# The gate phase of PEER: started 32 gathered rows earlier on VectorE, with two of three steps' gated comparison made by ScalarE

## What is computed

```
s = einsum('thcd,hcnd->thcn', q, sub_keys)            # 8 heads, 2 halves, 128 keys
s_top, i_top = top_k(s, 16)                           # then top 16 of the 256 sums
best_s, best_pos = top_k(cand_s, 16)
expert = take_along_axis(cand_e, best_pos)            # i0 * 128 + i1, out of 16384
gate = softmax(best_s)
act = gelu(einsum('td,thkd->thk', x, u[expert]))
y = einsum('thk,thkd->td', gate * act, v[expert])
```

## Time and profile before

| | us |
|---|---|
| median of 3 runs | 5255.7 |
| lowest, highest | 5235.42, 5274.73 |
| profiled execution, its own time | 5254.98 |
| span of its trace, first to last instruction | 5253.1 |

### The profile page before, as it was taken

One profiled execution on the slowest core, in us unless ns is written; L12 is line 12 of the kernel. 1 busy time (PEld: TensorE's weight loads), 2 busy tenths in 40 slices (PEclk: granted clock), 3 DMA queues, 4 the chain that ended last, 5 costly groups with the idle time before them and its releaser, 6 DMA issues. The chain is left out here.

```text
span 5253.1 us, 56097 instructions
## 1 busy us (share of the span) xinstructions
PE 4308.1 (82%) x21158; PEld 3533.7 (67%) x21158; DVE 3096.9 (59%) x5685; ACT 1026.1 (20%) x2272; POOL 1920.2 (37%) x1559
## 2 busy tenths in 40 slices
PE   6989679788997559996787799996888997469995
PEld 5467438577886458885555688863677886458884
DVE  1315540599957796656216633345599867796656
ACT  0102310222332150000012222211222332150000
POOL 0000230166657624444002433312256557614444
PEclk9985669899998779998878788858899998779997
DMA  2330112488889948998111000013588889939998
GB/s 91 89 75 1 34 37 96 167 301 313 311 338 397 369 128 342 409 396 348 56 58 35 1 1 1 1 41 104 188 300 310 319 341 390 363 109 371 409 399 333
DMA packets 403487, 1099.26 MB, mean 209 GB/s; under 512 B 70508, under 2 KB 157261, under 8 KB 402886
## 3 DMA queue, kind: packets, MB, share of 16 engines
q0 software_dynamic: 186496, 679.04, 34.4%
q1 hardware_dynamic: 216726, 416.69, 22.6%
HBM read 1066.88 MB, written 32.45 MB: 209 GB/s over the span
## 5 line engine op out<-in xcount | busy, mean ns | idle before, releaser
L1036 DVE SCALAR_TENSOR_TENSOR gg_ytok<-gg_ring,gg_gw,gg_ytok 128x1024 f32<-128x1024 f32 x320 | 422.1, 1319 | 178.5 <-DMA gg_ring<-in_peer_v,gg_idx 172.5
L1036 DVE SCALAR_TENSOR_TENSOR fg_ytok<-fg_ring,fg_gw,fg_ytok 128x1024 f32<-128x1024 f32 x320 | 422.0, 1319 | 176.6 <-DMA fg_ring<-in_peer_v,fg_idx 170.0
L706 POOL DMA_INDIRECT fg_ring<-in_peer_u,fg_idx x320 | 377.2, 1179 | 351.7 <-DVE fg_ring L1030 284.4
L706 POOL DMA_INDIRECT gg_ring<-in_peer_u,gg_idx x320 | 374.4, 1170 | 345.7 <-DVE gg_ring L1030 275.9
L1030 DVE SCALAR_TENSOR_TENSOR fg_ring<-fg_ring,fg_htok 128x1024 f32<-128x1024 f32 x320 | 409.7, 1285 | 128.1 <-DMA fg_ring<-in_peer_u,fg_idx 126.4
L1030 DVE SCALAR_TENSOR_TENSOR gg_ring<-gg_ring,gg_htok 128x1024 f32<-128x1024 f32 x320 | 409.8, 1286 | 127.8 <-DMA gg_ring<-in_peer_u,gg_idx 125.7
L774 PE MATMUL fg_bank<-f_hTd,fg_uT 128*128 128x256 f32 x2048 | 476.9, 387 | 0.6 <-ACT f_buf L873 0.6
L774 PE MATMUL gg_bank<-g_hTd,gg_uT 128*128 128x256 f32 x2048 | 476.2, 387 | 0.6 <-ACT g_buf L873 0.6
L706 POOL DMA_INDIRECT gg_ring<-in_peer_v,gg_idx x320 | 358.1, 1119 | 272.1 <-DVE gg_ytok L1036 211.8
L706 POOL DMA_INDIRECT fg_ring<-in_peer_v,fg_idx x320 | 345.7, 1080 | 276.3 <-DVE fg_ytok L1036 214.4
L774 PEld LDWEIGHTS fg_bank<-f_hTd,fg_uT 128*128 128x128 f32 x2048 | 389.8, 196 | 51.2 <-issue 0.9
(11 more groups left out here) (620 smaller groups left out, 7758.8 us busy)
## 6 DMA issues: line engine op xcount, KB each, us to landing
fg_ub<-in_peer_u SPq DMA_DIRECT2D x128, 512.0 KB, 6.8
gg_ub<-in_peer_u SPq DMA_DIRECT2D x128, 512.0 KB, 6.7
fg_ub<-in_peer_v SPq DMA_DIRECT2D x64, 512.0 KB, 7.2
fg_uT<-in_peer_v SPq DMA_DIRECT2D x64, 512.0 KB, 6.7
gg_ub<-in_peer_v SPq DMA_DIRECT2D x64, 512.0 KB, 7.3
gg_uT<-in_peer_v SPq DMA_DIRECT2D x64, 512.0 KB, 6.8
f_buf<-in_peer_w_q SPq DMA_DIRECT2D x16, 1024.0 KB, 12.2
g_buf<-in_peer_w_q SPq DMA_DIRECT2D x16, 1024.0 KB, 11.8
```

Source lines behind the costliest of these rows:

```text
L706: pool.indirect_dma_start(ring[:, n % RING, :], None, (u_rows if kind == "u" else v_rows)[:, :], bass.IndirectOffsetOnAxis(ap=idx[:, r:r + ...
L1036: dve.scalar_tensor_tensor(ytok[:, :], row, gw[:, r:r + 1], ytok[:, :], ALU.mult, ALU.add).then_inc(used, 1)
```

## The change

Four edits, all in PEER. `UNITS_U` falls from 370 to 338, so the gate phase stands 32 gathered units earlier in DVE's order, and 32 more units stand after it. `place` uses 30 us in place of 25 for the Gelu over dots. In steps with `t % 3 != 2` (22 of 32) DVE makes only the first comparison; ACT builds the second one with its gate: eight `Abs` (distance of `iota128` from the index, L896 in the changed file) and, after a wait for its own writes, eight `Relu` of gate minus gate times distance (L902), which is the gate where the distance is 0 and 0 elsewhere. For that `selT` gets a fourth part, the negated gate. PE waits for both DVE and ACT before a step.

```diff
-UNITS_U = 370
+UNITS_U = 338
...
-        selT = ph.sb("selT", [P, 3, TD])
+        selT = ph.sb("selT", [P, 4, TD])
...
+        def by_act(t):
+            return t % 3 != 2
...
-        for c, k in zip(early_chunks, place(sched, [dots_at[c] for c in early_chunks], 25.0)):
+        for c, k in zip(early_chunks, place(sched, [dots_at[c] for c in early_chunks], 30.0)):
...
                 for t in range(NGC):
                     pe.wait_ge(og_done, t + 1)
+                    pe.wait_ge(oh_done, t + 1)
...
-                    act.activation(selT[:, :, i * P:(i + 1) * P], acc[:, i, 0:3 * P].rearrange("p (a t) -> p a t", a=3),
-                                   ACT.Copy).then_inc(sT_done, 1)
+                    act.activation(selT[:, 0:3, i * P:(i + 1) * P], acc[:, i, 0:3 * P].rearrange("p (a t) -> p a t", a=3),
+                                   ACT.Copy)
+                    act.activation(selT[:, 3, i * P:(i + 1) * P], acc[:, i, 2 * P:3 * P], ACT.Copy, scale=-1.0
+                                   ).then_inc(sT_done, 1)
...
-                    act.wait_ge(oh_done, t + 1)
-                    for k in range(GT):
-                        a = oh[t % 2][:, 1, k, :]
-                        last = act.activation(a, a, ACT.Copy, scale=selT[:, 2, t * GT + k:t * GT + k + 1])
-                    last.then_inc(og_done, 1)
+                    if by_act(t):
+                        if t >= 2:
+                            act.wait_ge(gm_done, t - 1)
+                        elif t == 0:
+                            act.wait_ge(g_done, nblk)
+                        for k in range(GT):
+                            last = act.activation(oh[t % 2][:, 1, k, :], iota128, ACT.Abs, scale=-1.0,
+                                                  bias=selT[:, 1, t * GT + k:t * GT + k + 1])
+                        last.then_inc(ab_done, 1)
+                        act.wait_ge(ab_done, sum(by_act(x) for x in range(t + 1)))
+                        for k in range(GT):
+                            a, col = oh[t % 2][:, 1, k, :], slice(t * GT + k, t * GT + k + 1)
+                            last = act.activation(a, a, ACT.Relu, scale=selT[:, 3, col], bias=selT[:, 2, col])
+                        last.then_inc(og_done, 1)
+                    else:
...
-                    for a in range(2):
+                    for a in range(1 if by_act(t) else 2):
```

More of the change, by code:

```diff
@@ L523, in peer_layer @@
                                                          ph.sem("hit_done"), ph.sem("look_done"))
-        idx_done, gate_done, sT_mm, sT_done = ph.sem("idx_done"), ph.sem("gate_done"), ph.sem("sT_mm"), ph.sem("sT_done")
+        idx_done, gate_done, sT_mm, sT_done, ab_done = ph.sem("idx_done"), ph.sem("gate_done"), ph.sem("sT_mm"), ph.sem("sT_done"), ph.sem("ab_done")
         t_half, e_half, h_done, g_done = ph.sem("t_half"), ph.sem("e_half"), ph.sem("h_done"), ph.sem("g_done")
@@ L883, in _ @@
                 for t in range(NGC):
-                    act.wait_ge(oh_done, t + 1)
-                    for k in range(GT):
-                        a = oh[t % 2][:, 1, k, :]
-                        last = act.activation(a, a, ACT.Copy, scale=selT[:, 2, t * GT + k:t * GT + k + 1])
-                    last.then_inc(og_done, 1)
+                    if by_act(t):
[13 more added lines that the diff above has]
+                    else:
+                        act.wait_ge(oh_done, t + 1)
+                        for k in range(GT):
+                            a = oh[t % 2][:, 1, k, :]
+                            last = act.activation(a, a, ACT.Copy, scale=selT[:, 2, t * GT + k:t * GT + k + 1])
+                        last.then_inc(og_done, 1)
                     while late and at["u", late[0] * CHUNK_R + CHUNK_R - 1] < UNITS_U + PER_GC * t:
```

## The result

| | before | after |
|---|---|---|
| median, us (22 runs each) | 5279.86 | 5293.49 |
| lowest, highest | 5235.42, 5286.0 | 5276.83, 5304.95 |
| profiled execution, own time | 5254.98 | 5294.56 |

The ratio is 1.0029, with a 95% interval of 1.0016 to 1.0042: some 15 us slower, a loss so small that it takes 22 runs of each to see it. The median lies inside the forecast range of 5212 to 5300 us, and the difference within the 1% that the prediction called no change. The profiled execution of before stands 25 us under the median of before, so the two traces differ by more (39.5 us of span) than the two kernels do. Of these 39.5 us, 20.9 arise ahead of the first PEER, in code that is the same in both: the first PEER starts at 961.8 us in the one and at 982.7 in the other.

What follows compares the result with a forecast made beforehand. The DMA engines' gathers bound the kernel nearly everywhere but the gate phase. Per layer: start -44.8, gate +4.3 or +1.9, tail +44.8; both layers 5255.0 + 6.2 = 5261 us, range 5212 to 5300.

Steps and rivals of the forecast that it cites:

- The start: Ahead of the gate phase: DVE's first comparison comes near 1796 us, 44.8 us sooner than 1840.76, per layer.
- The eleven blocks: Unit phase after the Gelu of chunk 10: eleven blocks without a wait, 4.32 us each, take 47.5 us.
- The rival in which the unit phase doesn't end sooner: Blocks run at 5.7 us, `selT` comes as before, 15 us lost per layer: 5291 us; chance 0.11.
- The tail: After the output phase: 61 gathered units left where 29 were; the 32 more cost 44.8 us per layer.
- the upper price of 1.49: Mean us per gathered unit after the output matmuls, including loads of x; 1.40 was taken, range 42.2 to 47.7 us.
- The rival in which PE ends the layer: All 270 remaining units fit beside the output matmuls; each layer ends 45 us sooner, 5165 us in all; chance 0.06.
- The gate phase: Paced by a loop through DVE, ACT and PE: 160 us, +4.3 in the first PEER, +1.9 in the second.
- m = 3.2: Gate phase: us taken for PE's passes in the loop, expected more often slow than not; range 2.05 to 3.78.
- The duration of `Relu` that the prediction had to bound: Gate phase on ACT: second per-partition operand adds 0 to 180 ns, 90 taken; eight `Relu` last 3.16 us.
- 11.8 + m: Gate phase: us per three steps for multiplication, comparisons, scaling, `Abs`, `Relu`, four hand-overs and PE's passes; 15.0 taken.
- DVE's saved comparisons: Gate phase: 22 comparisons fewer on DVE, 25 us, end as waits for PE and ACT, some 30 us.
- The rival of a shorter gate phase: `Relu` costs as much as the scaling, passes mostly fast: gate phase 140 us, 5216 us in all; chance 0.17.

Runs made afterwards that it cites:

- before with two units: The kernel before with two gathered units per gate step in place of one, without the split and with 370 units ahead: ratio 0.9993 (0.9973 to 1.0013).
- the kernel with three units per step: The changed kernel with ACT building all 32 steps, `Relu` with the gate as only per-partition operand, three gathered units per step: ratio 0.9826, median 5175.93 us.
- the cheaper `Relu`: The changed kernel with `Relu` of fixed scale -1.0 and the gate as bias, its only per-partition operand: ratio 0.9971 (0.9951 to 0.9991).
- two per step: The changed kernel with two gathered units per gate step in place of one: ratio 0.9877 (0.9822 to 0.9931).
- DVE's order: The changed kernel with DVE comparing before it multiplies for steps that ACT does not build: 5268.74 us in a single execution.

## Why the prediction was right, and what was mis-sized

*The start* (-44.8): right. -46.5 and -44.9; the first comparison came at 1815.2 - 20.9 = 1794.3 on the clock of before, where 1796 was forecast, and ACT waited for dots last at 1740.9 there. The eleven blocks took 47.5 us as reckoned. The rival in which the unit phase doesn't end sooner is out.

*The tail* (+44.8): right in its mechanism, 3 us small. The output phase holds 209 units at a DMA share of 1.02, whether it starts early or late, and 61 stand behind it. The 32 came at 47.4 / 32 = 1.48 us, near the upper price of 1.49, not at 1.40. The rival in which PE ends the layer is out for this change; it came true in before with two units and in the kernel with three units per step, where units were moved into the gate phase and not to its other side.

*The gate phase* (+4.3 and +1.9): the right sign and the right loop, 3 to 4 us small each: +7.1 and +5.6. The sign hung on the choice of m = 3.2, which was an estimate; with the mean pass time of before, 2.78, the same loop gives 155.5 us and no growth. The closing passes measured 3.03 and 3.08 us in the mean of ten turns of each gate phase, so here the choice was lucky as well as reasoned. The duration of `Relu` that the prediction had to bound came out as taken. The rows of ACT by line, before:

```profile
L902 ACT ACTIVATE fg_misc<-fg_misc,fg_selT 128x128 f32<-128x128 f32 x88 | 35.0, 480 | 0.4
L896 ACT ACTIVATE gg_uT<-top_cm,gg_selT 128x128 f32<-128x128 f32 x88 | 26.8, 387 | 1.8 <-PE gg_bank L804 1.8
L896 ACT ACTIVATE fg_misc<-top_cm,fg_selT 128x128 f32<-128x128 f32 x88 | 26.8, 387 | 2.8 <-PE fg_bank L804 2.8
L896 ACT ACTIVATE fg_uT<-top_cm,fg_selT 128x128 f32<-128x128 f32 x88 | 26.8, 387 | 1.2 <-PE fg_bank L804 1.1
L896 ACT ACTIVATE gg_misc<-top_cm,gg_selT 128x128 f32<-128x128 f32 x88 | 26.8, 386 | 0.3 <-PE gg_bank L804 0.3
```

480 - 387 = 93 ns for the second operand. By the rule of the Trainium skill ("ScalarE: Activation LUTs", section "What ACT_TABLE_LOAD costs") it is about 93 for each; the trace agrees.

The term that was short is the loop taken for the whole phase: 11.8 + m per three steps with m = 3.2, so 15.0, times 32/3. The phase of 162.8 us comes to 15.3 per three steps. Two parts of the term were a little dear. The ten turns of the first gate phase take from 13.66 to 16.72 us, and five of them are 11.62 plus their own passes to 0.02 us (passes of 2.05 three times, 2.93 and 3.79): 11.62 where 11.8 was reckoned. The passes that close the ten turns took 3.03 us in the mean where 3.2 was taken.

Two things were left out. The first is a wait: `Abs` of step t + 3 writes the buffer that PE reads for step t + 1, and must wait until those passes are done. The other five turns are longer by it, up to 1.4 us each and 4.5 us together. It is one row of the timeline:

```profile
1837.36 3.43 PE L804 MATMUL fg_bank<-fg_uT 128*128 128x128 f32 x16 [3.50 <-ACT fg_uT L902]
...
1840.83 2.45 ACT L896 ACTIVATE fg_uT<-top_cm,fg_selT 128x128 f32<-128x128 f32 x8 [0.97 <-PE fg_bank L804]
```

ACT stands 0.97 us until the passes that began at 1837.36 are done. In the groups above ACT waits there 1.1 + 2.8 us in the first gate phase and 1.8 + 0.3 in the second. So a slow set of passes can cost in two places of the turn. The two do not add up: in all twenty turns of the two gate phases the excess is what the passes of step t + 1 take beyond those of step t, less 0.30 us, and nothing where that is below 0. A slow set right after a fast one is what costs.

The second thing left out is the two ends of the phase. Ten turns are 30 steps; the two steps that remain took 11.8 us in the first gate phase (5.0 up to the first multiplication, 6.8 from the end of the last turn) where 10.0 were reckoned; DVE waits 4.3 us there for the passes of the last step. In the second gate phase they took 14.2, with such a wait of 6.1. The first phase is 151.0 + 11.8, against 150 + 10; in the second the turns took 149.6 us, 2.6 of them that wait, and the whole excess lies at the ends.

With the cheaper `Relu` these groups wait 0.0 us, and its turns are the plain loop, 10.88 + m to 0.2 us, with passes of 2.05 or about 3.5. Its ten turns take 136.9 us where those of after take 151.0. That is the 14 us: 7.4 of `Relu`, 2.5 of closing passes (2.78 in the mean in place of 3.03), and 4.2 of this wait. A third buffer, which would take the wait alone away, was not tried.

DVE's saved comparisons did end as waits, as forecast, for some 39 us where 30 were expected (columns: us in total, times, longest):

```profile
DVE g_buf L1075 <- PE gg_bank L804: 39.7, 23, 6.1
DVE f_buf L1075 <- PE fg_bank L804: 38.7, 22, 4.3
```

The rival of a shorter gate phase named the right condition: with `Relu` at the price of a scaling and faster passes, the phase does fall below that of before. That kernel measured 0.9971.

Together the PEERs of the two traces grew by 18.3 us where +6.2 was forecast: 6.5 more in the gate phases, 5.2 in the tails, 2.2 in the rest, less 1.8 by earlier starts. By the medians the growth is 13.6. The forecast of 5261 us stands on a profiled execution 25 us under the median of 22 runs; the same +6.2 on that median would be 5286. So where the measured median falls in the range says more of that baseline than of the change, whose growth was a little over twice the forecast. What the 20.9 us ahead of the first PEER are was not tried: kernels with the same code up to there began it anywhere between 961 and 985 us.

## What to carry to other kernels

Where one resource is full in every stage but one, starting that stage earlier may be worth nothing, as it was here: ask instead how much of the full resource's work can be put into it. Taking work from the busiest engine of a stage helps only if the time it frees is filled, here with gathered units (two per step: -1.2%, three: -1.7%), and only until another engine ends the layer. And a loop through several engines must be written out with the waits for buffers as well as those for data, since a slow member may be in two of them.

## What the runs showed that was not expected

The same 512 passes of a gate phase are not the same time in any two kernels. In after a set of 16 that takes 2.05 us (at 1855.90) has a granted clock of 1.00, one that takes 3.79 (at 1861.46) of 0.50: the two levels, 2.4 and 1.2 GHz. In first gate phases:

| kernel | phase, us | passes, us | granted clock |
|---|---|---|---|
| cheaper `Relu` | 148.8 | 85.02 | 0.82 |
| before | 155.7 | 89.09 | 0.78 |
| DVE's order | 159.3 | 99.84 | 0.68 |
| after | 162.8 | 97.81 | 0.72 |
| all by ACT, three units | 186.7 | 105.32 | 0.65 |

The longer the phase, the slower the passes, but for one case. The table does not say which is the cause: between before and after the passes grew by 8.7 us and the phase by 7.1, and since passes are part of the loop, slower passes lengthen the phase as well. The mean time between sets does not order the kernels: it is (148.8 - 85.02) / 32 = 1.99 us with the cheaper `Relu`, 2.08 before, 2.03 after, and 1.86 with DVE's order, which has nearly the lowest clock. Whether the clock follows from the length of a step or from how the pauses are spread in it, no run tells apart, since none changed the pauses alone; so the mean of PE's passes could not have been reckoned from the trace of before to better than some tenths of a microsecond a step.
